# Two square sums from one pass over the residual, and the bias store moved into the recurrence

## The reference

```
def rms_norm(x, w):
    y = x * rsqrt(mean(x * x) + 1e-6);  return y * w
x = x + gt2 * conv_ffn(h, ...)          # end of the first block; w_down is its last product
x = rms_norm(x, norm_f_w)               # end of the first block
# second block
h = rms_norm(x, g_mix) * (1 + sc1) + sh1
z = h @ w_in_2                          # queries, keys and values of two attentions, and gates
...
o_b = chunk_band_attend(q_b, k_b, v_b, rel_bias)   # adds a bias by relative position
x = x + gt1 * (merged @ w_out)
```

## Time and profile before

| | |
|---|---|
| median of 3 runs | 2397.83 us (2397.09 to 2399.01) |
| the profiled execution | 2400.04 us, its span 2398.2 us |
| mean granted TensorE clock | 0.968 |
| busy: TensorE, its weight loads | 92%, 66% |
| busy: VectorE, ScalarE, POOL | 48%, 30%, 9% |
| chain that ended last | TensorE 79%, VectorE 8%, DMA 6%, ScalarE 4% |

### The profile page before, as it was taken

How to read it: one execution, slowest core, us unless ns; L and a number is a source line. 1 busy time by engine, 2 the same in 40 slices (tenths; PEclk the granted TensorE clock), 3 DMA queues, 4 the chain that set the end, 5 groups by cost and what they waited for, 6 DMA issues and landing times.

```text
span 2398.2 us, 41197 instructions
## 1 busy us (share of the span) xinstructions
PE 2210.3 (92%) x17720; PEld 1572.6 (66%) x17720; DVE 1142.6 (48%) x2011; ACT 710.7 (30%) x1086; POOL 217.9 (9%) x97
## 2 busy tenths in 40 slices
PE   7989898989989999988989999989899999799994
PEld 5485858585436889665668888857655677456563
DVE  4545454553756555245567773252355643511113
ACT  2323222321221222344353332242134532322221
POOL 0020202020000000000124344410000000000001
PEclk9999999999989999999999999989999999899997
DMA  8201010102547556101323332345120133579994
GB/s 256 83 9 37 20 37 20 36 21 83 158 153 231 178 182 200 38 1 48 111 82 94 87 104 80 97 80 145 31 79 19 45 110 96 206 288 397 398 412 171
DMA packets 216314, 295.26 MB, mean 123 GB/s; under 512 B 7640, under 2 KB 191872, under 8 KB 207968
## 3 DMA queue, kind: packets, MB, share of 16 engines
q1 hardware_dynamic: 210784, 274.85, 33.9%
q0 software_dynamic: 3072, 9.74, 2.0%
q10 hardware_dynamic: 2304, 8.39, 0.9%
HBM read 279.84 MB, written 13.11 MB: 122 GB/s over the span
## 4 chain that ended last, share of the span: by engine, by line
PE 79%; DVE 8%; DMA 6%; ACT 4%; issue 2%; SPq 1%; POOL 0%; POOLq 0%; DVEq 0%; ACTq 0%
PE ps L661 11%; PE ps L1148 10%; PE ps L766 10%; PE ps L989 8%; PE ps L957 6%; PE ps L1179 5%; PE ps L1359 4%; DMA ring<-in_w_up 3%; PE ps L1013 3%; PE ps L1043 2%; PE ps L870 2%; PE ps L1059 2%; PE ps L1332 2%; PE ps L1130 2%; PE ps L1206 2%
## 5 line engine op out<-in xcount | busy, mean ns | idle before, releaser
L766 PE MATMUL ps<-arena 64*64 64x64 f32 x7168 | 227.3, 222 | 15.4 <-POOL arena L1915 8.8
L766 PEld LDWEIGHTS ps<-arena 64*64 64x64 f32 x7168 | 222.3, 138 | 20.0 <-POOL arena L1915 9.6
L661 PE MATMUL ps<-hT,ring 128*128 128x512 f32 (+1 forms) x480 | 213.0, 600 | 3.1 <-ACT hT L1431 2.4
L1921 POOL TENSOR_TENSOR w_low<-ring,w_high 128x2048 fp32r<-128x2048 f32 x22 | 101.8, 4627 | 817.0 <-ACT w_high L1674 817.0
L661 PEld LDWEIGHTS ps<-hT,ring 128*128 128x128 f32 (+1 forms) x480 | 90.0, 189 | 120.4 <-issue 117.7
L1148 PE MATMUL ps<-h_high,w_low 128*128 128x512 f32 x352 | 140.8, 400 | 5.7 <-DVE h_low L2336 5.7
L1148 PE MATMUL ps<-h_high,w_high 128*128 128x512 f32 x352 | 140.8, 400 | 0.0
L1148 PE MATMUL ps<-h_low,w_high 128*128 128x512 f32 x352 | 139.3, 396 | 0.0
L2242 DVE CUSTOM_DVE_ANT_0 arena<-ps,arena 128x256 f32<-128x256 f32 (+3 forms) x160 | 67.0, 468 | 124.5 <-PE ps L1059 124.4
L1457 ACT ACTIVATE arena<-ps 128x512 f32<-128x512 f32 x104 | 62.1, 597 | 209.7 <-PE ps L766 199.4
L2059 DVE TENSOR_TENSOR arena<-ps,arena 128x512 f32<-128x512 f32 x88 | 60.8, 691 | 119.1 <-PE ps L766 119.0
(11 more groups left out here) (408 smaller groups left out, 4362.6 us busy)
## 6 DMA issues: line engine op xcount, KB each, us to landing
ring<-in_w_in SPq DMA_DIRECT2D x54, 1024.0 KB, 5.3
arena<-in_w_ada SPq DMA_DIRECT2D x80, 512.0 KB, 4.2
arena<-in_w_down SPq DMA_DIRECT2D x32, 1024.0 KB, 9.3
ring<-in_w_gate SPq DMA_DIRECT2D x30, 1024.0 KB, 9.8
ring<-in_w_up SPq DMA_DIRECT2D x30, 1024.0 KB, 11.2
ring<-in_w_up SPq DMA_DIRECT2D x44, 512.0 KB, 4.9
ring<-in_w_down SPq DMA_DIRECT2D x8, 1024.0 KB, 5.1
y_scratch<-arena ACTq DMA_DIRECT2D x16, 512.0 KB, 7.4
```

The source lines that it names most:

```text
L661: mm = pe.matmul(dst, w[:, k, hf * P:hf * P + width], rhs(k), start=(start and k == 0), stop=(stop and k == kts - 1))
L766: mm = pe.matmul(ps[r, bank, cc], l[r, cc], x[r, 0:64] if x is eye64 else x[r, cc], start=(i == 0), stop=(i == len(terms) - 1))
L1921: pool.tensor_tensor(W_LOW[:, slot_, :], ring[:, slot_, :], W_HIGH[:, j % 2, :].bitcast(F32), ALU.subtract).then_inc(w_low, 1)
```

## The change

Five things are changed.

1. ScalarE squares each residual tile of w_down twice, once weighted by |`norm_f_w`| (made at the start as the Sqrt of its square) and once plain (`square_both`). VectorE keeps two running sums (`add_both`), and TensorE sums both over the partitions. The weighted sum gives the root for in2's input directly; `norm_f_w` goes into `GAIN`.
2. The plain sum gives a second root, `RSTD_F`, made after in2's input. With it VectorE scales the carried residual (`carry`), one tile after each of its copies in in2.
3. The splits of in2's first two weight blocks move into the w_down phase, with buffers of their own.
4. The bias row is loaded, widened and stored in two halves of 320 columns, at the head of POOL's four rounds in the recurrence. The read into `BT` stays where it was, but waits for nothing that is new there.
5. The new Ln and Exp pairs have no line that names a table set.

```diff
         H4_HIGH, H4_LOW = [rounded("h4_" + n, offset_of["arena"] + at * 4, KT, T) for n, at in (("high", 6656), ("low", 10752))]
-        IN2_W_HIGH = [rounded(f"in2_w_high_{i}", offset_of["arena"] + at * 4, SLOT)[:, :] for i, at in enumerate((14848, 28672))]
+        IN2_W_HIGH = [rounded(f"in2_w_high_{i}", offset_of["arena"] + at * 4, SLOT)[:, :] for i, at in enumerate((18944, 20992, 14848, 28672))]
...
             size = SLOT // 2 if i == 2 else SLOT
-            return m, IN2_W_HIGH[i % 2][:, 0:size], ring[:, m % R, 0:size], W_LOW[:, m % R, 0:size]
+            return m, IN2_W_HIGH[i if i < 2 else 2 + i % 2][:, 0:size], ring[:, m % R, 0:size], W_LOW[:, m % R, 0:size]
...
         EPSC, GNC, ZERO, ONE, ZSINK = [small[:, i:i + 1] for i in range(5)]
+        EPS_SQUARED = small[:, 16:17]
+        WEIGHED = small[:, 80:88]
+        SQUARES = area(16896, 4, T)
+        RSTD_F = area(34304, T)
         NM, DEN = [small[:, at:at + 4].rearrange("p (a b) -> p a b", b=2) for at in (6, 10)]
...
         PLS = [small[:, 64:72], small[:, 72:80]]
-        ZERO8 = small[:, 80:88]
         RSTD = sb("rstd", [P, T])[:, :]
+        BIAS_ROW = sb("bias_row_half", [P, 320])[0:8, :]
...
         squares_added = sem("squares_added")
-        ADDED_AT = {1: 0, 2: KT - 1, 4: 2 * (KT - 1)}
+        ADDED_AT = {1: 0, 2: KT - 1, 4: 3 * (KT - 1)}
+        SQUARED_AT = {0: 0, 1: KT, 2: 2 * KT, 4: 4 * KT, 5: 5 * KT}
         norm_scaled, norm_applied = sem("norm_scaled"), sem("norm_applied")
-        SCALED_AT, APPLIED_AT = {1: 0, 3: 8, 4: 16}, {1: 0, 2: 8, 3: 16, 4: 24}
+        SCALED_AT, APPLIED_AT = {1: 0, 3: 8, 4: 16}, {1: 0, 3: 8, 2: 16, 4: 24}
         h_high, w_high, w_low = [sem(n) for n in ("h_high_made", "weights_high_made", "weights_low_made")]
...
                 for k in range(first, last):
-                    pe.wait_ge(squared, KT * k_norm + k + 1)
+                    pe.wait_ge(squared, SQUARED_AT[k_norm] + k + 1)
                     mm = pe.matmul(ps[:, 6, :], ones, hT[:, k, :], start=(k == 0), stop=(k == KT - 1))
...
-            def norm_total(k_norm):
-                pe.wait_ge(squares_added, ADDED_AT[k_norm] + KT - 1)
+            def norm_total(k_norm, added=None):
+                pe.wait_ge(squares_added, added or ADDED_AT[k_norm] + KT - 1)
                 pe.matmul(ps[:, 6, :], ones, hT[:, 0, :], start=True, stop=True).then_inc(summed, 1)
...
                         mm.then_inc(half_done, 1)
-            norm_total(2)
+            pe.wait_ge(squares_added, ADDED_AT[2] + 2 * (KT - 1) - 1)
+            pe.matmul(ps[:, 7, :], ones, SQUARES[:, 0, :], start=True, stop=True).then_inc(summed, 1)
+            norm_total(2, ADDED_AT[2] + 2 * (KT - 1))
...
-            norm_sum(3)
             drain_psum(pe, "in2")
...
             act.wait_ge(consts_made, 1)
+            lg(act.activation(WEIGHED, WEIGHED, ACT.Sqrt, bias=EPSC))
             act.wait_ge(got_x, 16)
...
                 up_silu(jj, *ident_)
-            for d in range(2, 12):
-                down_weights_high(d)
-                for k in range(2 * (d // 3) - 2, 2 * (d // 3)) if d % 3 == 1 else ():
-                    norm_square(k, freed["D"], BEFORE["down"]["D"] + k + 1)
-            for k in (6, 7):
-                norm_square(k, freed["D"], BEFORE["down"]["D"] + k + 1)
-            norm_root(2)
-            if stop < 5:
-                return
-            for k in range(KT):
-                norm_square(k, norm_applied, APPLIED_AT[2] + k + 1)
+            def square_both(k):
+                act.wait_ge(freed["D"], BEFORE["down"]["D"] + k + 1)
+                if k >= 4:
+                    act.wait_ge(squares_added, ADDED_AT[2] + 2 * (k - 3) - 1)
+                act.activation(SQUARES[:, 1 + (k - 1) % 3 if k else 0, :], xT[:, k, :], ACT.Square,
+                               scale=WEIGHED[:, k:k + 1]).then_inc(squared, 1)
+                act.activation(hT[:, k, :], xT[:, k, :], ACT.Square).then_inc(squared, 1)
...
+            for d in range(2, 12):
+                down_weights_high(d)
+                for k in range(2 * (d // 3) - 2, 2 * (d // 3)) if d % 3 == 1 else ():
+                    square_both(k)
             in2_weight_high(0)
             in2_weight_high(1)
-            norm_root(3)
+            for k in (6, 7):
+                square_both(k)
+            act.wait_ge(summed, 3)
+            lg.done(act.activation(RSTD, ps[:, 7, :], ACT.Ln, scale=1.0 / D, bias=EPS_SQUARED))
+            act.activation(RSTD, RSTD, ACT.Exp, scale=-0.5, bias=ZERO).then_inc(rooted, 1)
+            if stop < 5:
+                return
             h_value = [0] * KT
...
                     act.activation(H4_HIGH[:, k - 1, :], hT[:, k - 1, :], ACT.Copy).then_inc(h4_high, 1)
+            act.wait_ge(summed, 4)
+            lg.done(act.activation(RSTD_F, ps[:, 6, :], ACT.Ln, scale=1.0 / D, bias=EPSC))
+            act.activation(RSTD_F, RSTD_F, ACT.Exp, scale=-0.5, bias=ZERO).then_inc(rooted, 1)
             act.wait_ge(angled, 1)
...
                 return
+            def bias_part(q):
+                if q == 0:
+                    pool.dma_start(BIAS_ROW[:, 255:320], a["rel_reversed"][:, 0:65]).then_inc(bias_row, 16)
+                if q == 1:
+                    pool.wait_ge(bias_row, 16)
+                    pool.tensor_copy(BIAS_ROW[:, 0:255], BIAS_ROW[:, 255:256].broadcast_to([8, 255])).then_inc(pool_link, 1)
+                    pool.wait_ge(pool_link, 1)
+                    pool.dma_start(a["bias_scratch"][:, :, 0:320], BIAS_ROW.unsqueeze(1).broadcast_to([8, P, 320])).then_inc(bias_out, 16)
+                if q == 2:
+                    pool.wait_ge(bias_out, 16)
+                    pool.dma_start(BIAS_ROW, a["rel_reversed"][:, 65:385]).then_inc(bias_row, 16)
+                if q == 3:
+                    pool.wait_ge(bias_row, 32)
+                    pool.dma_start(a["bias_scratch"][:, :, 320:640], BIAS_ROW.unsqueeze(1).broadcast_to([8, P, 320])).then_inc(bias_out, 16)
             np_ = len(PRODUCTS)
             for q in range(4):
+                bias_part(q)
                 for li, b in enumerate(LEVELS):
...
             pool.wait_ge(freed["D"], BEFORE["in2"]["D"])
-            pool.dma_start(BROW[0:8, 255:640], a["rel_reversed"][:, 0:385]).then_inc(bias_row, 16)
             pool.dma_start(CH, a["consts"][:, CONST_AT["chunked"][0]:CONST_AT["chunked"][0] + T]).then_inc(got_pos, 16)
             pool.dma_start(ANG[:, 3, :].bitcast(I32), a["positions"].partition_broadcast(P)).then_inc(got_pos, 16)
-            pool.wait_ge(bias_row, 16)
-            pool.tensor_copy(BROW[0:8, 0:255], BROW[0:8, 255:256].broadcast_to([8, 255])).then_inc(pool_link, 1)
-            pool.wait_ge(pool_link, 1)
-            pool.dma_start(a["bias_scratch"], BROW[0:8, :].unsqueeze(1).broadcast_to([8, P, 640])).then_inc(bias_out, 16)
-            pool.wait_ge(bias_out, 16)
+            pool.wait_ge(bias_out, 32)
...
             lk(dve.memset(GNC, GN_EPS))
+            lk(dve.memset(EPS_SQUARED, EPS * EPS))
             dve.memset(ZERO, 0.0).then_inc(dve_link, 1)
...
+            lk.done(tt(WEIGHED, col("norm_f_w", 0, 8), col("norm_f_w", 0, 8), ALU.mult))
             lk.done(ts(OMU, col("mu", 0, 27), -1.0, 1.0, ALU.mult, ALU.add))
...
-                dve.wait_ge(squared, KT * k_norm + k + 1)
+                dve.wait_ge(squared, SQUARED_AT[k_norm] + k + 1)
                 if k >= 2:
...
                 tt(hT[:, 0, :], hT[:, 0, :], hT[:, k, :], ALU.add).then_inc(squares_added, 1)
+            def add_both(k):
+                for i, (total, square) in enumerate(((SQUARES[:, 0, :], SQUARES[:, 1 + (k - 1) % 3, :]), (hT[:, 0, :], hT[:, k, :]))):
+                    dve.wait_ge(squared, SQUARED_AT[2] + 2 * k + i + 1)
+                    if k >= 2:
+                        dve.wait_ge(squares_added, ADDED_AT[2] + 2 * (k - 2) + i + 1)
+                    tt(total, total, square, ALU.add).then_inc(squares_added, 1)
+            def in2_weight_low(i):
+                if i >= 9:
+                    return
+                _, high, full_, low = in2_weight(i)
+                dve.wait_ge(in2_w_high, i + 1)
+                tt(low, full_, high.bitcast(F32), ALU.subtract).then_inc(in2_w_low, 1)
...
                     if i >= 2:
-                        add_square(k_norm, i - 1)
-                add_square(k_norm, 7)
+                        add_both(i - 1) if phase == "down" else add_square(k_norm, i - 1)
+                    if phase == "down" and i == 5:
+                        in2_weight_low(0)
+                        in2_weight_low(1)
+                add_both(7) if phase == "down" else add_square(k_norm, 7)
...
             residual("down", mod[:, 40:48], 2)
-            dve.wait_ge(rooted, 3)
-            for k in range(KT):
-                stt(xT[:, k, :], xT[:, k, :], col("norm_f_w", k), RSTD, ALU.mult, ALU.mult).then_inc(norm_applied, 1)
             if stop < 5:
...
             gain(mod2, 0, col("g_mix_2", 0, 8))
-            def in2_weight_low(i):
```

(16 more changed lines are left out.)

## The result

| | |
|---|---|
| after, median of 5 runs | 2415.22 us (2407.41 to 2427.02) |
| before, on the same chip, median of 5 | 2399.01 us (2397.09 to 2400.28) |
| ratio | 1.0073 [1.0042, 1.0104] |
| predicted | 2376.9 us, 2373.5 to 2383.5 |
| the profiled execution of after | 2407.41 us, its span 2405.6 us |

The account below looks back on a forecast made before the run. TensorE was taken to carry most of the chain, so other engines' work counts only where TensorE idles. Savings 10.9 + 5.8 + 2.9 + 1.3 = 20.9 us from the median 2397.83 gave 2376.9 us, range 2373.5 to 2383.5.

Parts of the forecast that it names:

- Recurrence: Bias store moved there in two halves; the next ring load should still be in time: nothing, or a few us.
- rival 4: Recurrence: instruction fetch starves beside the store; 2.5 us at each of 13 packets gives 2409.4; slower 0.05, 0.02 more for cancelling.
- 1.2 us each: Recurrence: engine time read per instruction packet, 9 packets in 40 us at 1.7% of 16 engines.
- under the store in in2 TensorE kept its 0.2333 spacing: Argument against fetch starving in the recurrence: in2's matmuls kept pace under the store, though with fewer instructions per us.
- the ring load of 29.38 us under the store: Seam and in2: a 1024 KB ring load that otherwise took 5.5 us took five times that during the bias store.
- Seam: Between w_down and the second block's in2: scaling starts at 1586.78 instead of 1597.63, 10.9 us saved.
- The length of a half: Recurrence: half of the bias store takes 27.8 us by bytes or 55.6 by rows; 27.8 taken.
- rival 3: Seam: a switch of table set costs more than its load, adding 1.4, so 2378.3 us; chance 0.05.
- in2: Second block's in2: ring load stall falls, 5.8 us saved, and the slow clock after it, 2.9 saved.
- The carry, the late root, the splits and the doubled adds: Seam's covers, in w_down and in2: work moved into idle time of VectorE and ScalarE, expected to cost nothing.
- Start: Kernel start: the early Sqrt brings a table in, so squares start earlier; 1.3 us saved, bounds 0 and 1.3.
- The sum: Whole kernel: savings of seam, in2 and start together, 10.9 + 5.8 + 2.9 + 1.3 = 20.9 us.

Follow-up runs that it names:

- e1: Changed kernel, each half of the bias store issued only when the last product of the round before is done: 2381.26 us, ratio 0.9920.
- e3: Kernel before with the bias edit alone, loaded, widened and stored in halves in the recurrence: 2425.88 us, ratio 1.0101.
- e10: Kernel before with all of the change but the bias, which keeps its old place and narrow store: 2399.46 us, ratio 0.9997.
- e5: Changed kernel with stores waiting for the round's head, plus the line naming the table set before both new Ln and Exp pairs: 2383.87 us, ratio 0.9920.
- e8: Kernel before with the bias store in its old place, but from 128 partitions instead of eight: 2395.91 us, ratio 0.9970.
- e2: Changed kernel without the two stores and their waits, BT read from weight tensor w_in: 2380.42 us, ratio 0.9906.
- e11: Kernel before with the norm edits, the table set named, and the bias store in its old place from 128 partitions: 2381.51 us, ratio 0.9930.
- e7: Changed kernel, each half of the store copied DRAM to DRAM from weight tensor w_in: 2379.12 us, ratio 0.9899.
- e9: Changed kernel with the bias row on 16 partitions instead of eight, same time of issue: 2405.65 us, ratio 1.0032.

## Why the prediction was wrong

One step failed: **Recurrence: "Nothing, or a few us"**. It came to +31.1 us, waits of 23.7 more and matmuls at a lower granted clock behind them. e1 and e3 show it from both sides: the bias moved alone costs 1.0%, and the same move with the stores 30 us later costs nothing. The step priced only the next ring load, which was indeed in time.

The mechanism stood in rival 4, at 0.05. One reading set its size, the other was all that stood against it:

- *"1.2 us each"*. That is how long a packet takes once it is served, and the delays that the rival tried, 1.0 to 2.5 us each, are of that size. What counts is how long it waits, and no share of busy time tells. Under the store the packet still took 1.1 us, and TensorE waited 13.2 for it.
- *"under the store in in2 TensorE kept its 0.2333 spacing"*. It did, but there the instruction queue brought 4 packets in 165 us (1560 to 1725 of before), one in 41, against one in 4.4 in the recurrence. A delay of 13 us can be hidden in the first and not in the second. The prediction noted "fewer instructions per us" and didn't work out the factor, 9.

And the row that would have told was quoted: the ring load of 29.38 us under the store. Issued at 1616.55 it ended at 1645.9, 3 us after POOL had seen the store done (1642.91). The prediction read it as a transfer slowed fivefold. e10 shows that half of it waits for the store's end. Read so, a fetch packet issued under a store of 30 us could be due 10 us and more late, and the sum is the 25 us from which rival 4 decides. The rival's own form, 13 delays of 2.5 us, was wrong as well: there were three waits, of 13.2, 6.9 and 4.4 us.

Right, and how near:

- *Seam*: 10.9 predicted, 17.42 - 6.63 = 10.8 measured. The adds cost 0.40 more before the first Ln (3.77 after the last residual tile against 3.37), where 0.45 was taken. The second table load of 1.28 between Ln and Exp was there; the line that names the set takes it out (e5).
- *The length of a half*: 27.8 predicted, 29.7 and 30.8 measured.
- *A drain of 1.4 behind a switch of set* (rival 3): no. Ln to Exp is 0.72 us without the switch (e5) and 2.00 with it, 1.28 more.
- *in2*: 8.7 predicted; 19.3 less 10.8 is 8.5. e3 has it alone at 8.8 in its trace, e8 at 0.9970.
- *The carry, the late root, the splits and the doubled adds*: free as said. The splits ran at 1593.98 (3.90) and 1598.16 (2.29), before tile 6 at 1606.00. An add held by POOL took 4.61 us at 1582.02, far from the chain's end.
- *Start*: 1.3 predicted, 1.9 in this pair of traces. But the chain now runs through a load of `w_ada` of 16.84 us that ends at 38.09, and the start differs between executions: 45.0 to 45.9 us in the eleven with the early Sqrt, 45.9, 46.0 and 47.0 in the three without. It is worth nearer 0.5 to 1; in 0.2% it can't be told.
- *The sum*: 20.9, and 22 measured in e2, where the stores are gone; the other cured kernels lie 16.6 (e11) to 24.5 us (e7) below before.

The prediction also took the sum to be one of independent parts. They are not: e10 loses 8.6 of the seam's 10.8 us again to the ring load that the narrow store holds. In2's term stands by itself (e3, e8); the seam's needs the narrow store gone from there.

**Open.** How the store holds back the packets of other queues: that a packet waits where it meets an engine of the store fits the rows. Under the narrow store, at a share of one half, half of each ring load passed and half was held, and some instruction packets passed and some waited; under e9's, with all 16 engines at work, no instruction packet passed. But no run here shows which engine a packet goes to, nor why one that meets the store waits for its end and not for one packet of it. And the packet near 423.8, 17 us behind the last, came in the middle of the store, neither at its usual time nor at the store's end. Why a packet of the store takes 0.8 us from 8 or 16 partitions and 0.23 from 128 or from DRAM is open too (fewer partitions, or the same row read more often), and so is the spread of the changed kernel's runs.

## What to carry to other kernels

A long transfer from few SBUF partitions has to be placed by who else needs the DMA engines during its time, and an engine that runs small instructions is one: look at how many packets per us its instruction queue moves, not at their share of busy time. Better still, make the transfer short: the same 1280 KB took 30 us from 8 partitions, 15.6 from 16 and 6.0 to 6.6 from 128. When one stall sets a fixed time, as the store did for in2's ring load, work saved ahead of it is lost in it, so edits are to be tried together and apart.

## What the runs showed of the hardware

- A store with 8 source partitions moved 49 GB/s at a share of 0.49; one with 16, 5 KB packets of 0.81 us at a share near 0.97; one with 128 partitions about 360 GB/s; DRAM to DRAM took 6.3 us for 1280 KB.
- Ring loads that met a narrow store landed 1.7 to 3.3 us after it (e10, before, e1), after half of their bytes had moved in the first 5 us (e10, before). TensorE's instruction packet that was held came with the store's end (near 187.2 and 436.7 in after, 174.6 in e9), though its own engine time was 1.1 us, and TensorE went on some 2.4 us behind it.
- TensorE ran 64 x 64 matmuls at 0.031 us each and needed a 16 KB instruction packet for every 125 of them, each with its weight load: one per 4.4 us. It had some 6 us of them in hand when the supply stopped (last packet near 406.7, wait from 412.91).
- ACT_TABLE_LOAD cost 1.28 us, with the next ACTIVATE 0.01 us behind it.
